# Hybrid retention and HGRN2 encoder step on 8 cores: two more x tiles loaded into the output tiles' buffers, and later landings assumed in the ordering

## The chip, the cores and the metric

The kernel runs on all 8 cores of one Trainium2 chip. Each core takes one of the 8 prompt streams and two of the 16 sample streams; the cores don't exchange data. The metric is device time in microseconds (us) of the slowest core, from the first to the last instruction and what lies around them. Lower is better.

## What is computed

One layer. For each of the 8 prompts (2048 frames of 1024 numbers) and 16 samples (16 frames each, with a running state):

```python
h = rmsnorm(x, g_pre)
u = h @ w_in                      # 1024 x 4096: eight segments of 512
rq, rk, rv, rg, hq, hf, hi, hg = split(u)
# head group A, retention, 4 heads of 128: rotary q and k, decay gamma per head
# head group B, HGRN2, 4 heads of 128: f = lb + (1-lb)*sigmoid(hf), k = 1-f, v = hi, q = silu(hq)
#   both: S_t = decay_t * S_(t-1) + k_t v_t^T,  o_t = q_t S_t, computed in chunks
o = concat(silu(rg) * headnorm(o_r), silu(hg) * headnorm(o_h))
y = x + rmsnorm(o @ w_out, g_post)
```

Outputs: y for prompts and samples, and the final states of both head groups.

## The kernel before, in words

**Tiling.** A core works on 16 prompt tiles of 128 frames, in four blocks of four tiles, and one sample tile of 48 rows (two streams of 16 frames at rows 0 and 32). All weights are held in SBUF as bf16: `Wi` (input, loaded by ten DMAs on GpSimd's queue at line 603 in the order of segments 0-1, 2-3, 4-5, 6-7) and `Wo` (output, two DMAs behind them). Most operations are recorded by name in these stages:

- `stage_A(k, j)` (line 648) for tile j of block k: x is loaded into a buffer by SP (line 662), ScalarE squares and sums it (line 670), GpSimd adds epsilon and takes the power (lines 673, 676), VectorE writes the normed tile `xbf` (line 679), and this is transposed into `xT`, on TensorE with a copy by ScalarE (lines 693, 697) in blocks 0 and 1, by a DMA transpose (line 685) in blocks 2 and 3. `xT` has two buffers, one a block.
- `stage_B_hg(k, h)` (line 753), head h of the HGRN2 group for a whole block: the projection of segment 5 (line 714), two ScalarE passes (lines 766, 768), forward scans on VectorE (line 773), a difference on GpSimd (line 781, `KTh`), more scans (line 785), the projection of segment 4, its SiLU (line 789) and a product on GpSimd (line 791, `QTh`). The scans' buffers `fG` and `fR` are double, `fQ` is single.
- `tile(k, j)` (line 1080): the rotary table's load, `stage_B_ret` (retention q and k: projections at line 731, rotary on VectorE, sums on GpSimd), `stage_C` (values and gates), `stage_D` (scores, outputs, state update; states `Sst` and `Sb`), `stage_E` (output projection at line 1009, norm, result in `xr`, stored by SP at line 1048). For all tiles but the last two `stage_E` lets a DMA of GpSimd's queue add x into `xr` (line 1031).

**The buffers in question.** x tiles are counted over the whole program, i = 0 to 16. `xs` and `xr` have two buffers each of 512 KB. Tile i goes to `xs[i % 2]`; only i = 2 and 3 go to `xr`, which `stage_E` otherwise uses for its results. So of block 1 (i = 4 to 7) tile 6 can be loaded only when tile 4 has been read, tile 7 when tile 5 has been read. The loads i = 4 and 5 also wait for the second half of segments 4 and 5 of `Wi` (key `('Wi', 5, 3)`).

**What sets the order.** The recorded order only gives the dependences (who writes and reads which name). The order of each engine's instructions, and of the DMAs that SP issues, is then chosen by a list scheduler (`list_schedule`, line 197) while the program is built. It keeps a planned time: each operation has a modelled cost and latency, a DMA is put through a model of the two queues (class `Net`), and at each step the operation that can start first is placed; among those that could start within 300 ns, the one with the higher priority (the longest chain behind it, plus a boost for early loads, plus noise of up to 500 from the seed `S.jitter`). PSUM banks are given out there too. When a DMA's modelled transfer ends, `landed` (line 250) makes its successors ready. On the chip nothing of the planned time is left, only the order on each engine and the semaphore waits: an engine that reaches an instruction whose data is not there stands, with all that is behind it.

`front(k)` (line 1065) records `stage_A` of the block's four tiles, the small set-up, and `stage_B_hg` for four heads; then the block's tiles follow. Block 1's `stage_A` is therefore recorded behind block 0's last `stage_E`. Filler matmuls (line 1128) are put into planned gaps of TensorE in the first 16 us.

Of the kernel before, what the change touches and what calls it, by code (L numbers as in the profile page):

```python
# [12 lines left out]
PE, ACT, DVE, POOL, SP = "pe", "act", "dve", "pool", "sp"  # L13
# [15 lines left out]
class Bank:  # L29
    def __init__(self, reserve):  # L30
        self.reserve = reserve
        self.idx = 0
# [45 lines left out]
class Sched:  # L78
    def __init__(self):
        self.ops = []  # L80
        self.last_w = {}
        self.readers = {}
        self.jitter = None

    def op(self, eng, fn, reads=(), writes=(), dma_key=None, deps=()):
        oid = len(self.ops)
        d = set(deps)
        for b in reads:
            w = self.last_w.get(b)
            if w is not None:  # L90
                d.add(w)
        for b in writes:
            w = self.last_w.get(b)
            if w is not None:
                d.add(w)
            d.update(self.readers.get(b, ()))
        d.discard(oid)
        self.ops.append(dict(eng=eng, fn=fn, deps=d, dma_key=dma_key, sig=False, sem=None, val=0, line=sys._getframe(1).f_lineno,
                             writes=tuple(writes), banks=[b for b in dict.fromkeys(tuple(reads) + tuple(writes)) if isinstance(b, Bank)]))
        for b in reads:  # L100
            self.readers.setdefault(b, []).append(oid)
        for b in writes:
            self.last_w[b] = oid
            self.readers[b] = []
        return oid
# [91 lines left out]
    def list_schedule(self):  # L197
# [16 lines left out]
        for i in range(n - 1, -1, -1):  # L214
            o = ops[i]
# [11 lines left out]
        XLAT = 110.0  # L227
# [5 lines left out]
        ready_t = [0.0] * n  # L233
# [16 lines left out]
        def landed(until):  # L250
            out = net.advance(until)
            for i, t in out:
                o = ops[i]
                t += o["lat"]
                o["t_land"] = t
                for sx in succ[i]:
                    ready_t[sx] = max(ready_t[sx], t + XLAT)
                    ndeps[sx] -= 1
                    if ndeps[sx] == 0:
                        avail[ops[sx]["eng"]].append(sx)  # L260
            return len(out)

        while done < n:
            best = None
            for e in ENGS:
# [4 lines left out]
                for i in avail[e]:  # L270
# [4 lines left out]
                    if v is not None:  # L275
                        k = free_bank(v)
# [15 lines left out]
            if landed(best[2] if best is not None else None):  # L292
                continue
# [4 lines left out]
            e, i, st_ = best  # L298
            o = ops[i]
            v = o["allocs"]  # L300
            if v is not None:
                k = free_bank(v)
# [189 lines left out]
def build_nc(limit=None, marks=None):  # L492
# [28 lines left out]
    with ExitStack() as st:  # L521
# [58 lines left out]
        def pbb(v):  # L580
            return psum[v.idx][:].bitcast(BF16)

        S = Sched()
# [64 lines left out]
        def stage_A(k, j):  # L648
            i = nA[0]
            nA[0] += 1  # L650
            slot = i % 2
            L = k.rows
            xbuf, xkey = xs[slot], ("xs", slot)
            if i in (2, 3):
                xbuf, xkey = xr[slot], ("xr", slot)
            if k.sample:
                S.op(POOL, lambda e: e.memset(xbuf[0:LS, :], 0.0), writes=[xkey])
                S.op(SP, lambda e: e.dma_start(out=xbuf[0:16, :], in_=xsm[0:16, :]), writes=[xkey], dma_key=("xsm", 0))
                S.op(SP, lambda e: e.dma_start(out=xbuf[32:48, :], in_=xsm[16:32, :]), writes=[xkey], dma_key=("xsm", 1))
            else:  # L660
                t0 = (k.b * 4 + j) * 128
                xid = S.op(SP, lambda e: e.dma_start(out=xbuf[:], in_=xp[t0:t0 + 128, :]), writes=[xkey], dma_key=xkey)
                if i < 4:
                    S.ops[xid]["boost"] = 20e6 - 1e6 * i
                elif i < 6:
                    S.ops[xid]["deps"].add(S.last_w[('Wi', 5, 3)])
            n0 = len(S.ops)
            junk, jk = (xbf[slot], [("xbf", slot)]) if i >= 4 else (gate[i], [("gate", i, 0), ("gate", i, 512)])
            sq = i % 4
            S.op(ACT, lambda e: e.activation(out=junk[0:L, :], in_=xbuf[0:L, :], func=AF.Square, scale=1.0 / 32,  # L670
                                             accum_out=ssx[0:L, sq:sq + 1]),
                 reads=[xkey], writes=[("ssx", sq)] + jk)
            S.op(POOL, lambda e: e.tensor_scalar(out=ssx[0:L, sq:sq + 1], in0=ssx[0:L, sq:sq + 1],
                                                scalar1=EPS, scalar2=None, op0=ALU.add),
                 reads=[("ssx", sq)], writes=[("ssx", sq)])
            S.op(POOL, lambda e: e.tensor_tensor(out=rsx[0:L, sq:sq + 1], in0=ssx[0:L, sq:sq + 1],  # L676
                                                 in1=mhalf[0:L, 0:1], op=ALU.pow),
                 reads=[("ssx", sq), "mhalf"], writes=[("rsx", sq)])
            S.op(DVE, lambda e: e.scalar_tensor_tensor(out=xbf[slot][0:L, :], in0=xbuf[0:L, :], scalar=rsx[0:L, sq:sq + 1],  # L679
                                                       in1=gpre[0:L, :], op0=ALU.mult, op1=ALU.mult),  # L680
                 reads=[xkey, ("rsx", sq), "gpre"], writes=[("xbf", slot)])
            if i == 3:
                first_norms.append(len(S.ops) - 1)
            if (k.b >= 2 and not k.sample):
                S.op(SP, lambda e: e.dma_start_transpose(out=k.xT[:, :, j * 128:(j + 1) * 128], in_=xbf[slot][:, :]),
                     reads=[("xbf", slot)], writes=[("xT", k.par, j)], dma_key=("xtr", slot))
            else:
                T = S.bank()

                def tr(e):  # L690
                    ins = None
                    for kc in range(8):
                        ins = e.transpose(out=pbb(T)[:, kc * L:(kc + 1) * L], in_=xbf[slot][0:L, kc * 128:(kc + 1) * 128],
                                          identity=ident[0:L, 0:L])
                    return ins
                S.op(PE, tr, reads=[("xbf", slot), "ident"], writes=[T, ("xT", k.par, j)])
                S.op(ACT, lambda e: e.activation(out=k.xT[:, :, j * 128:j * 128 + L],  # L697
                                                 in_=pbb(T)[:, 0:8 * L].rearrange("p (k l) -> p k l", k=8), func=AF.Copy),
                     reads=[T], writes=[("xT", k.par, j)])
            if i < 4:  # L700
                for o in S.ops[n0:]:
                    o["boost"] = 9e6 - 1e5 * i
# [34 lines left out]
        def lb_chain():  # L737
            S.op(DVE, lambda e: e.tensor_tensor(out=lbd[:], in0=lbt[:, 0, :], in1=lbt[:, 1, :], op=ALU.subtract),
                 reads=["lbt"], writes=["lbd"], deps=first_norms)
            S.op(ACT, lambda e: e.activation(out=lbd[:], in_=lbd[:], func=AF.Tanh, scale=0.5), reads=["lbd"], writes=["lbd"])  # L740
            S.op(DVE, lambda e: e.tensor_scalar(out=lbc[:, 0, :], in0=lbd[:], scalar1=0.25, scalar2=0.75, op0=ALU.mult, op1=ALU.add),
                 reads=["lbd"], writes=["lbc0"])
            S.op(DVE, lambda e: e.tensor_scalar(out=lbc[:, 1, :], in0=lbd[:], scalar1=-0.25, scalar2=0.25, op0=ALU.mult, op1=ALU.add),
                 reads=["lbd"], writes=["lbc1"])
# [312 lines left out]
        blocks = [prompt_block(b) for b in range(4)]  # L1057
# [5 lines left out]
            return rid  # L1063

        def front(k):
            for j in range(k.ns):
                stage_A(k, j)
            if k.b == 0:
                lb_chain()
            if k.sample or k.b < 2:  # L1070
                set_ret_dec(k)
            if k.sample:
                for i in range(NF):
                    S.op(POOL, lambda e, i=i: e.memset(fG[i][:, 0:2, 16:17], 1.0), writes=[("fG", i)] + [("fG", i, c) for c in range(1, 4)])
                S.op(POOL, lambda e: e.memset(k.QT[:, :, 0:LS], 0.0), writes=[("QT", k.par, h) for h in range(4)])
                S.op(POOL, lambda e: e.memset(k.KT[:, 0, :, 0:LS], 0.0), writes=[("KT", k.par, h) for h in range(4)])
            for h in range(4):
                stage_B_hg(k, h)
# [47 lines left out]

        def filler_fn(e, k):
            return e.matmul(psum[k][:, 0:128], lhsT=ident[:], rhs=ident[:], start=True, stop=True)
        S.jitter = (13, 500.0)
        S.emit(nc, st, filler=(filler_fn, ident_ready, 700.0, 400.0, 60.0, 16000.0, 1300.0, 6))  # L1130
    return nc

# [64 lines left out]
```

How the kernel before makes its waits and increments, by code:

```python
            def then_inc(self, *a, **k):  # L109
                return self
# [336 lines left out]
        def run(h, e):  # L447
            waited = {}
            for i in streams[e]:
                o = ops[i]
                req = {}
                for dpi in need[i]:
                    dp = ops[dpi]
                    key = id(dp["sem"])
                    if key not in req or req[key][1] < dp["val"]:
                        req[key] = (dp["sem"], dp["val"])
                for key, (sem, val) in req.items():
                    if waited.get(key, 0) >= val:
                        continue
                    h.wait_ge(sem, val)
                    waited[key] = val
                ins = o["fn"](h)
                if o["sig"]:
                    ins.then_inc(o["sem"], 16 if o["dma_key"] is not None else 1)
```

## Time and profile before

| | us |
|---|---|
| three runs | 381.78, 383.2, 438.44 |
| median | 383.2 |
| the profiled execution: time | 382.71 |
| its span on the slowest core (core 7) | 381.2 |
| spans of the 8 cores | 377.5 to 381.2 |
| TensorE, matmuls: busy | 357.4 (94%) |
| VectorE, ScalarE, GpSimd: busy | 237.9, 183.9, 218.7 |
| mean granted TensorE clock, core 7 | 0.991 |

One execution is profiled; the rows below are of its slowest core, in us from the span's start. PE is TensorE's matmuls, PEld its weight loads, DVE VectorE, ACT ScalarE, POOL GpSimd, SP the engine that issues most DMAs (SPq its queue). Matmuls overlap, so that the busy time of one is longer than what it adds to the total. A bracket behind a row of the timeline is the idle time of the engine just before it and what ended it.

### The profile page before, as it was taken

The numbers are of one execution on the slowest core, as the hardware profiler recorded it, in microseconds if no ns is written. First come the engines' busy times: TensorE is split into PE (matmuls) and PEld (weight loads), VectorE is DVE, ScalarE is ACT, GpSimd is POOL, SyncE is SP. The second block draws the span as 40 slices with busy tenths as digits, with TensorE's granted clock in tenths as the row PEclk, the third lists the DMA queues.
The fourth block names the chain that finished last, engine by engine and source line by source line (L and its number), as shares of the span: only waits on it lengthen the run. The fifth ranks groups of instructions, "written<-read, shape, count | busy, mean of one in ns | idle before, by whom it ended". The sixth has DMA issues, their size and how long they took to land.

```text
span 381.2 us, 8011 instructions; the slowest of 8 cores (377.5 to 381.2 us)
## 1 busy us (share of the span) xinstructions
PE 357.4 (94%) x2375; PEld 188.7 (50%) x2375; DVE 237.9 (62%) x524; ACT 183.9 (48%) x567; POOL 218.7 (57%) x292
## 2 busy tenths in 40 slices
PE   8989699689999999999979999999999999999993
PEld 8844354335455555444535454545454555545541
DVE  0137464684986975968656749486666464477545
ACT  2431242857878745463535252626353425435551
POOL 8425542557578776657446756575746365364630
PEclk9999899999999999999999999999999999999999
DMA  7999999997090997664566472525352556466714
GB/s 197 204 172 171 176 162 209 179 245 169 0 147 23 230 200 174 164 116 119 115 147 123 124 150 56 137 59 131 62 131 55 129 95 101 80 138 145 213 36 125
DMA packets 60619, 51.56 MB, mean 135 GB/s; under 512 B 41632, under 2 KB 48832, under 8 KB 60576
## 3 DMA queue, kind: packets, MB, share of 16 engines
q1 hardware_dynamic: 53104, 32.69, 34.4%
q0 software_dynamic: 7472, 18.35, 30.9%
q8 instruction: 20, 0.33, 0.4%
q14 instruction: 23, 0.19, 0.2%
HBM read 41.73 MB, written 10.09 MB: 136 GB/s over the span
## 4 chain that ended last, share of the span: by engine, by line
PE 62%; DMA 21%; POOL 5%; issue 5%; ACT 3%; DVE 3%; DVEq 0%; POOLq 0%; SPq 0%; ACTq 0%
PE bank L731 33%; PE bank L1009 14%; DMA Wi<-w_in 13%; PE bank L714 8%; DMA xs<-xp 5%; DMA xs<-sret 2%; PE bank L927 2%; PE bank L932 2%; PE bank L944 2%; PE bank L895 1%; POOL Wi L603 1%; DMA xT<-xbf 1%; DVE xbf L679 1%; POOL QTh L791 1%; POOL rsx L676 1%
## 5 line engine op out<-in xcount | busy, mean ns | idle before, releaser
L731 PE MATMUL bank<-Wi,xT 128*128 128x512 bf16 (+1 forms) x816 | 190.1, 381 | 1.7 <-ACT xT L697 0.7
L731 PEld LDWEIGHTS bank<-Wi,xT 128*128 128x128 bf16 (+1 forms) x816 | 77.5, 99 | 86.2 <-issue 6.0
L714 PE MATMUL bank<-xT,Wi 128*128 128x512 bf16 (+1 forms) x320 | 62.5, 342 | 4.8 <-POOL QTh L791 2.4
L965 DVE SCALAR_TENSOR_TENSOR og<-bank,rsq,gate 128x128 bf16<-128x128 f32 (+1 forms) x136 | 38.6, 343 | 43.9 <-POOL rsq L962 27.0
L1009 PE MATMUL bank<-Wo,ogT 128*128 128x512 bf16 (+1 forms) x272 | 62.8, 379 | 2.5 <-DVE Sst L949 2.5
L714 PEld LDWEIGHTS bank<-xT,Wi 128*128 128x128 bf16 x320 | 26.6, 98 | 36.5 <-issue 9.8
L1009 PEld LDWEIGHTS bank<-Wo,ogT 128*128 128x128 bf16 (+1 forms) x272 | 25.9, 98 | 31.2 <-issue 3.0
L884 POOL TENSOR_TENSOR Sst<-Sst,decS 128x512 f32<-128x512 f32 x30 | 31.4, 1049 | 16.4 <-DVE Sst L949 11.5
L955 ACT ACTIVATE og<-bank 128x128 bf16<-128x128 f32 (+1 forms) x136 | 35.5, 281 | 5.7 <-PE bank L927 3.7
L962 POOL TENSOR_TENSOR rsq<-ssq,mhalf 128x4 f32<-128x4 f32 (+1 forms) x34 | 34.7, 1021 | 4.4
L888 ACT ACTIVATE Sb<-Sst 128x512 bf16<-128x512 f32 x30 | 18.9, 630 | 36.7 <-POOL Sst L884 16.3
L854 ACT ACTIVATE gate<-bank 128x512 bf16<-128x512 f32 (+1 forms) x34 | 20.3, 598 | 30.0 <-PE bank L731 29.7
L781 POOL TENSOR_TENSOR KTh<-fG 128x512 bf16<-128x512 f32 (+1 forms) x20 | 18.8, 942 | 27.6 <-DVE fG L773 27.6
L773 DVE TENSOR_TENSOR_SCAN fG<-bank,zer 128x128 f32<-128x128 f32 (+1 forms) x72 | 23.3, 378 | 17.3 <-ACT bank L768 15.6
L679 DVE SCALAR_TENSOR_TENSOR xbf<-xs,rsx,gpre 128x1024 bf16<-128x1024 f32 (+1 forms) x15 | 22.5, 1511 | 17.7 <-POOL rsx L676 17.7
L819 POOL TENSOR_TENSOR qtm<-tA,tB 128x512 bf16<-128x512 f32 (+1 forms) x17 | 22.7, 1338 | 16.2 <-DVE tA L806 12.0
L1013 ACT ACTIVATE og<-bank 128x512 bf16<-128x512 f32 (+1 forms) x34 | 20.2, 595 | 22.8 <-PE bank L1009 22.8
L785 DVE TENSOR_TENSOR_SCAN fR<-bank,inv,zer 128x128 f32<-128x128 f32 (+1 forms) x72 | 28.0, 439 | 2.1 <-DVE inv L777 0.6
L955 ACT ACTIVATION_READ_ACCUMULATOR og<-bank 128x1 f32 (+1 forms) x136 | 29.0, 214 | 0.0
L791 POOL TENSOR_TENSOR QTh<-fQ,fR 128x512 bf16<-128x512 f32 (+1 forms) x20 | 22.8, 1140 | 8.8 <-ACT fQ L789 4.0
L819 POOL TENSOR_TENSOR Ktr<-tA,tB 128x512 bf16<-128x512 f32 (+1 forms) x17 | 22.5, 1322 | 8.5 <-DVE tA L806 6.2
L1027 DVE SCALAR_TENSOR_TENSOR xr<-bank,rs,gpost 128x512 f32<-128x512 f32 x30 | 21.5, 742 | 9.2 <-PE bank L714 4.8
(97 smaller groups left out, 457.9 us busy)
## 6 DMA issues: line engine op xcount, KB each, us to landing
xr<-xp POOLq DMA_DIRECT2D x15, 512.0 KB, 6.1
yp<-xr SPq DMA_DIRECT2D x15, 512.0 KB, 3.6
xs<-xp SPq DMA_DIRECT2D x14, 512.0 KB, 7.0
Wi<-w_in POOLq DMA_DIRECT2D x6, 1024.0 KB, 45.6
Wi<-w_in POOLq DMA_DIRECT2D x4, 512.0 KB, 19.0
Wo<-w_out POOLq DMA_DIRECT2D x2, 1024.0 KB, 73.8
xr<-xp SPq DMA_DIRECT2D x3, 512.0 KB, 11.2
rot<-rot_p SPq DMA_DIRECT2D x16, 96.0 KB, 6.3
```

The lines of the kernel that those rows point to most:

```text
L679: S.op(DVE, lambda e: e.scalar_tensor_tensor(out=xbf[slot][0:L, :], in0=xbuf[0:L, :], scalar=rsx[0:L, sq:sq + 1], in1=gpre[0:L, :], op0=AL ...
L714: ins = e.matmul(pb(v)[:, 0:nt], lhsT=Wi[:, kc, col0:col0 + 128], rhs=k.xT[:, kc, 0:nt], start=(kc == 0), stop=(kc == 7))
L731: ins = e.matmul(pb(v)[0:L, :], lhsT=k.xT[:, kc, j * 128:j * 128 + L], rhs=Wi[:, kc, seg * 512:(seg + 1) * 512], start=(kc == 0), stop=(kc ...
L773: S.op(DVE, lambda e, c=c: e.tensor_tensor_scan(out=G[:, c, rsl(cl - 1, cl)], data0=pb(v)[:, rsl(c * st_ + cl - 1, cl)], data1=zer[:, 0:cl ...
L785: S.op(DVE, lambda e, c=c: e.tensor_tensor_scan(out=pack(R)[:, c, :], data0=pb(v)[:, c * st_:c * st_ + cl], data1=zer[:, 0:cl], initial=IV ...
L791: S.op(POOL, lambda e: e.tensor_tensor(out=tok(k.QT[:, h, :]), in0=pack(SQ), in1=pack(R), op=ALU.mult), reads=["fQ", ("fR", f)] + [("fR", ...
L819: S.op(POOL, lambda e, ts=ts, dst=dst: e.tensor_tensor(out=dst[0:L, :], in0=tA[ts][0:L, :], in1=tB[ts][0:L, :], op=ALU.add), reads=[("tA", ...
L884: S.op(POOL, lambda e, Sst=Sst, cc=cc, g=g, gsl=gsl: e.tensor_tensor(out=Sst[:, gsl].rearrange("p (h e) -> p h e", h=4), in0=Sst[:, gsl].r ...
L955: S.op(ACT, lambda e, q_=q_, h=h, vo=vo: e.activation(out=ogs[vs][0:L, h * 128:(h + 1) * 128], in_=pb(vo)[0:L, q_ * 128:(q_ + 1) * 128], f ...
L962: S.op(POOL, lambda e, gq=gq, g=g: e.tensor_tensor(out=rsq[vs][0:L, gq], in0=ssq[vs][0:L, gq], in1=mhalf[0:L, 0:4], op=ALU.pow), reads=[(" ...
L965: S.op(DVE, lambda e, q_=q_, h=h, vo=vo: e.scalar_tensor_tensor(out=ogs[vs][0:L, h * 128:(h + 1) * 128], in0=pb(vo)[0:L, q_ * 128:(q_ + 1) ...
L1009: ins = e.matmul(pb(y)[0:L, :], lhsT=ogT[:, kc, 0:L], rhs=Wo[:, kc, n * 512:(n + 1) * 512], start=(kc == 0), stop=(kc == 7))
```

## The change

Four edits, in `Sched`, `stage_A`, `front` and the end of `build_nc`. Tiles i = 6 and 7 are loaded into `xr[0]` and `xr[1]`. Their loads, like those of i = 4 and 5, wait for `('Wi', 5, 3)`. `stage_A` of block 1's four tiles is recorded right behind block 0's four, ahead of block 0's heads and outputs, so that in `xr` the x tiles 6 and 7 come before the results of block 0; `front` of block 1 no longer records them. In the scheduler, what depends on an operation of SP or on a DMA transpose becomes ready 3000 ns later in planned time. The seed of the noise goes from 13 to 10.

```diff
@@ class Sched, __init__
+        self.slack = 0.0
@@ list_schedule, landed
-                    ready_t[sx] = max(ready_t[sx], t + XLAT)
+                    ready_t[sx] = max(ready_t[sx], t + XLAT + (self.slack if o["eng"] == SP or o["tr"] else 0.0))
@@ stage_A
-            if i in (2, 3):
+            if i in (2, 3, 6, 7):
                 xbuf, xkey = xr[slot], ("xr", slot)
...
-                elif i < 6:
+                elif i < 8:
                     S.ops[xid]["deps"].add(S.last_w[('Wi', 5, 3)])
@@ front
-            for j in range(k.ns):
-                stage_A(k, j)
+            if k.b != 1:
+                for j in range(k.ns):
+                    stage_A(k, j)
             if k.b == 0:
+                for j in range(4):
+                    stage_A(blocks[1], j)
                 lb_chain()
@@ build_nc
-        S.jitter = (13, 500.0)
+        S.slack = 3000.0
+        S.jitter = (10, 500.0)
```

## Rows read from the trace of the kernel before

**Rows 1.** The page, part 1: busy us (share of the span) xinstructions
```profile
PE 357.4 (94%) x2375; PEld 188.7 (50%) x2375; DVE 237.9 (62%) x524; ACT 183.9 (48%) x567; POOL 218.7 (57%) x292
```

**Rows 2.** The chain that ended last, in order of time: start us, us, what
```profile
8.37 48.39 DMA Wi<-w_in
...
101.49 3.45 PE bank L714 x16
...
113.37 0.76 DVE xr L1027
...
179.81 8.20 DMA xs<-sret
...
370.97 3.62 PE bank L1009 x16
```

**Rows 3.** Groups by shape: busy us, mean ns of one, idle before and releasers
```profile
L731 PE MATMUL bank<-Wi,xT 128*128 128x512 bf16 x768 | 178.7, 381 | 1.7 <-ACT xT L697 0.7 <-DMA Wi<-w_in 0.6 <-DVE Sst L952 0.4
...
L714 PE MATMUL bank<-xT,Wi 128*128 128x512 bf16 x256 | 59.9, 381 | 4.8 <-POOL QTh L791 2.4 <-DVE fR L785 2.1 <-ACT V L851 0.3
```

**Rows 4.** Windows: length, busy us of PE, PEld, DVE, ACT, POOL, clock, DMA share, GB/s
```profile
60.00:80.00 20.00, 15.89 (x92) 7.46 (x90) 13.11 (x34) 12.03 (x20) 8.11 (x9) 1.00 1.06 205
...
200.00:240.00 40.00, 40.00 (x234) 20.10 (x233) 28.47 (x63) 17.07 (x59) 26.14 (x30) 1.00 0.55 113
```

**Rows 5.** Timeline of TensorE, 20 to 130 us: start us, us, instruction, idle before it
```profile
71.52 0.61 PE L693 MATMUL bank<-ident,xbf 128*128 128x128 bf16 x8 [0.86 <-DVE xbf L679]
74.23 1.89 PE L714 MATMUL bank<-xT,Wi 128*128 128x512 bf16 x8 [2.11 <-DVE fR L785]
...
83.87 1.89 PE L714 MATMUL bank<-xT,Wi 128*128 128x512 bf16 x8 [1.53 <-POOL QTh L791]
```

**Rows 6.** Timeline of all engines, 174 to 200 us
```profile
192.50 1.06 ACT L670 ACTIVATE xbf<-xs 48x1024 bf16<-48x1024 f32 x1 [3.29 <-DMA xT<-xbf]
...
197.02 1.89 PE L1009 MATMUL bank<-Wo,ogT 128*128 128x512 bf16 x8 [2.52 <-DVE Sst L949]
```

**Rows 7.** Timeline of all engines, 56 to 92 us
```profile
66.88 1.06 ACT L670 ACTIVATE xbf<-xs 128x1024 bf16<-128x1024 f32 x1 [3.20 <-DMA xs<-xp]
...
69.45 0.74 DVE L773 TENSOR_TENSOR_SCAN fG<-bank,zer 128x128 f32<-128x128 f32 x2 [4.03 <-ACT bank L768]
...
83.80 1.06 ACT L670 ACTIVATE xbf<-xs 128x1024 bf16<-128x1024 f32 x1 [1.72 <-DMA xs<-xp]
```

**Rows 8.** Timeline of SP's queue: the loads of x tiles 4 to 8
```profile
56.93 0.90 SPq L662 DMA_DIRECT2D xs<-xp  x2
...
71.55 0.33 SPq L662 DMA_DIRECT2D xs<-xp  x1
...
84.87 0.33 SPq L662 DMA_DIRECT2D xs<-xp  x1
```

**Rows 9.** SP's waits in 70 to 72 us: us in total, times, longest
```profile
SPq L460 <- DVE xbf L679: 13.5, 1, 13.5
```

**Rows 10.** DMA in 57.5 to 71.4 us (two rows), then 71.5 to 84 us
```profile
DMA packets 1185, 2.84 MB, mean 204 GB/s; under 512 B 62, under 2 KB 62, under 8 KB 1184
...
q1 hardware_dynamic: 288, 1.05, 24.5%
...
q1 hardware_dynamic: 343, 1.27, 30.6%
```

**Rows 11.** Tile Wo: its loads (ns, first and last start) and their landing
```profile
L603 POOL DMA_DIRECT2D Wo<-w_out x2: 777/781/785, 10.7 to 11.4; - x2
...
DMA to landing us min/median/max: 69.6/73.8/78.1
```

**Rows 12.** Tile Wi: its loads and their landing
```profile
L603 POOL DMA_DIRECT2D Wi<-w_in x10: 741/781/965, 2.0 to 9.9; - x10
...
DMA to landing us min/median/max: 14.1/33.6/62.2
```

## The prediction

> **What bounds the kernel now.** I read the page first. TensorE is busy for 94% of the span and no other engine is above 62% [rows 1], so TensorE sets the time and the question is where it lacks work. Busy time hides that, because matmuls overlap. Sixteen 512-wide matmuls in a row pass in 3.45 us in the chain [rows 2], 0.216 us each, while the busy column charges 381 ns for one [rows 3]. The 1024 full matmuls of the input projections [rows 3] are therefore 1024 x 0.216 = 221 us of streaming where the busy column has 238.6 us. So I walked TensorE's timeline and took for each group its start plus its count x 0.216 us (0.0555 us for a 128-wide one, from the same timeline); what is left to the next start is a gap.
>
> Outside four places there is none worth having. Of 200 to 240 us TensorE is busy for 40.00 of 40 us, of 60 to 80 us for 15.89 of 20 us [rows 4]. The gaps are:
> - up to 57 us: the order waits for weights. The last quarter of the third piece of the input weights lands at 56.8 us (8.37 + 48.39 us) [rows 2], and by then TensorE has done nearly all that needs no later piece. Whatever order is written, this part ends near 57 us.
> - 57 to 92 us: the three largest waits shown are 0.86, 2.11 and 1.53 us [rows 5]; with the latency hidden behind each, and the smaller ones, the gaps are 8 us.
> - 194.3 to 197.0 us: 2.7 us, shown as a wait of 2.52 us [rows 6].
> - the end: the last large group starts at 370.97 us [rows 2]; of it 1.0 us is gaps between dependent steps, and 6.6 us after it is a dependent tail that no order removes.
>
> With 0.5 us at 124 us that is about 12 us after 57 us that an order could give back, out of a profiled time of 382.7 us (span 381.2 us and 1.5 us around it). The median of the three runs is 383.2 us, 0.5 us above the profiled one.
>
> **What makes the gap at 57 to 92 us.** The heads of the HGRN2 part of block 0 are computed there: projection, two ScalarE passes, scans on VectorE, a product on GpSimd. ScalarE's next instruction in its order is the sum of squares of x tile i = 4 (the first of block 1), and it waits 3.20 us for that tile to land, until 66.88 us [rows 7]. The two passes of the next head stand behind it, VectorE idles 4.03 us for them [rows 7], and TensorE then runs short before 71.5 and 74.2 us [rows 5]. Before 83.80 us it waits again, 1.72 us, for the fourth tile [rows 7], and about as long before 80.25 us for the third. These were issued late: SP issues two loads at 56.93 us, then waits 13.5 us for the buffer of the first, and issues the third at 71.55 us [rows 8, 9].
>
> **Part 1, other buffers for tiles three and four of block 1.** Nothing is added in instructions or bytes: two 512 KB loads go to xr instead of xs. What goes is SP's wait of 13.5 us. They can be issued beside the first two at about 58 us. What is late next is the DMA engines: in 57.5 to 71.4 us the hardware queue moved 1.05 MB and in 71.5 to 84 us 1.27 MB [rows 10], 75 and 102 GB/s, beside the weights. Four tiles are 2.1 MB: at 75 GB/s the last lands at 57 + 28 = 85 us, at 102 GB/s at 57 + 20.6 = 77.6 us. Before it was about 83.8 us (the fourth's reader starts at 83.80 us as the tile lands). So the fourth tile moves between 1 us later and 6 us earlier; I take 2 us, nearer to the row with a short queue, since that is the row in which these loads would run. Tile three, by the same count, lands at 78 us in place of 80.2 us. What that is worth on TensorE: at least 0, since TensorE could be fed by the heads of block 0 alone, and at most the 2 us of gaps behind 80 us. I take 1 us.
>
> The Trainium skill, DMA: Bandwidth & Descriptors, section Queues, rings and completion order, says that each DMA engine goes round-robin between the queues it has work for, a packet at a time. By that rule a queue with four loads in it draws no larger share than one with two, the lower rate holds, and part 1 gives 0 us. The trace agrees only in part: the queue's share of the engines rose from 24.5% to 30.6% [rows 10] when more was in it.
>
> The block's outputs now write the buffers that these tiles hold. The first such write is at 113.37 us [rows 2], over 20 us after the tiles have been read: no cost. If that cover went, each us of lateness would go onto the output of tile 0, which TensorE does not wait for.
>
> The xs buffers come free earlier, so tiles one and two of block 2, loaded before from 84.87 us on [rows 8], can be loaded from about 71 us on. That is 1 MB more beside the last weights. The output weights, issued last at 11.4 us, take at most 78.1 us to land [rows 11], so 89.5 us; 1 MB at the 204 GB/s of 57.5 to 71.4 us [rows 10] would be 5 us. The first matmul that reads them runs at 107.6 us, so 0 on the path.
>
> **Part 2, the 3 us of slack.** It adds no instruction. Whatever follows a load, a store or a transpose issued by SP (not the adding DMAs of GpSimd's queue) is put later in its engine's order, behind work that is ready. Two measured stalls are of the kind that it moves. First, ScalarE's 3.20 us at 66.88 us and the smaller ones after it: if the sum of squares stands behind the next head's passes, the head chain goes on. That is worth between 0 and the 3.20 us plus 2 us behind; I take 3 us, near the row itself. Second, the 2.7 us at 194 us. There SP issues a state load at 179.81 us and stands 8.20 us for it [rows 2] before it issues the next into the same buffer; the transpose behind it on SP goes out late, ScalarE waits 3.29 us for it, and at the end of that chain TensorE 2.52 us [rows 6]. With landing planned later, the transpose, the output store and the next transpose would stand ahead of the second state load. I take 2 us of 2.7 us.
>
> **Part 3, the order drawn anew.** The noise seed, the slack and the earlier places in program order each change the whole order of 8011 instructions. No row prices this. The nearest are the present gaps: in 250 us of steady work one stall of 2.7 us and one of 0.5 us. Bounds: 3 us gained, if they go by luck, to two or three new stalls like the largest, 8 us lost. I take 2 us lost, a stall somewhat below the one seen.
>
> **Sum.** -1 - 3 - 2 + 2 = -4 us: 382.7 becomes 378.7 us in a profiled run, and 0.5 us more, rounded, 379 us as a median.
>
> **The rivals.**
> - Absorbed. The head chain of block 0 is bound by its own steps (two buffers for the scans, VectorE between them), so the waits of ScalarE only change their name, and the stall at 194 us turns up elsewhere. For it: TensorE waits for VectorE's scans for 2.11 us at 74.23 us [rows 5], not for x. Against it: the 4.03 us in which VectorE itself had nothing. It gives 382 to 384 us.
> - All of it. Every gap after 57 us but about 2 us goes, 10 us less: 373 us. For it: steady stretches are full already. Against it: the gaps at 57 to 92 us are a dependent chain while the weights still land.
> - Slower: weights crowded out. With four block 1 tiles at once and two of block 2 from 71 us on, up to three tiles' bytes (1.5 MB) run ahead of the last input weights. These were issued last at about 9.9 us and take at most 62.2 us [rows 12], so land at 72 us; 1.5 MB at 204 GB/s is 7.4 us. If they land after about 77 us, when TensorE has only those products left, it stalls for the rest, and one drawn stall comes on top: +5 us, up to +7.4 us, so 388 to 390 us. Against it: the hardware queue held a fairly steady share, so loads wait behind each other more than weights behind them.
> - The change doesn't do what it says: SP's order puts the two loads after something else that waits, and they go out at 70 us anyway. Then only parts 2 and 3 count: 380 us, within the forecast's own range.
>
> **How the numbers follow.** Forecast 0.50 (374.5 to 383 us), absorbed 0.20, all of it 0.13, crowded out 0.12, loads not early 0.05. The range that leaves out no more than two in ten runs from 372.5 to 388.5 us: down to all of it, up to most of the crowded case. A change of 2% (7.7 us) is about what a measurement of this kernel tells from none: faster than 375.5 us is all of it and the lower edge of the forecast, 0.17; slower than 390.9 us is the far end of the crowded case with new stalls, 0.10; the rest is 0.73.
>
> **What would show it.** Right: four loads of x issued by SP within about 3 us after 56.9 us with no 13.5 us wait; ScalarE without a wait over 1 us for x at 63 to 67 us; the product of the last head of block 0 (before at 86.7 us) some 3 us earlier; SP without an 8 us stand between state loads, and no TensorE gap there; steady stretches at 40.0 of 40 us. Wrong: the last quarter of the weights landing over 3 us later; or gaps of more than 3 us in all after 100 us, which would say that the drawn order costs more than the slack saves.

## The result, and the profile after

The changed kernel takes 378.07 us (median of 4 runs, 378.03 to 378.85) against 382.7 us before (381.78 to 383.2): a ratio of 0.988, 95% interval 0.986 to 0.990. One of the four runs before (438.44 us) was in the chip's slower state, at a lower granted clock, and is left out, as such runs are in every median below. The forecast was 379.0 us, 4 us less than before; 4.6 us less were measured. The sum was right and its terms came near in size, but the reason given for the largest fell, and that the redrawn order cost no more is luck.

The page of the changed kernel, parts 1 and 2 (line numbers are higher by 1 than before up to `front`):

```profile
span 376.5 us, 7940 instructions; the slowest of 8 cores (373.7 to 376.5 us)
...
PE 357.6 (95%) x2343; PEld 188.3 (50%) x2343; DVE 234.8 (62%) x524; ACT 183.5 (49%) x567; POOL 218.5 (58%) x292
...
PEclk9989799999999999999999999999999999999997
DMA  7999999999521979653958346362393464465407
```

Against [rows 1] the busy times are the same within 1.3%, and the 32 matmuls fewer are all fillers (203 against 235): no work was taken away. The page doesn't say where 4.7 us of span went. The windows do. First the kernel before, then the one after, for the 35 us behind the landing of the third piece of the input weights (columns as in rows 4):

```profile
57.00:92.00 35.00, 29.18 (x170) 14.02 (x169) 22.16 (x46) 19.11 (x33) 17.58 (x18) 0.98 0.99 205
```
```profile
57.00:92.00 35.00, 34.35 (x206) 17.08 (x204) 24.65 (x57) 23.84 (x47) 20.82 (x24) 1.00 1.07 217
```

TensorE begins 36 more matmuls in the same stretch. To put all kernels on one scale I keep a ledger for each core: the matmuls begun up to a time, without the fillers, the full ones at 0.216 us and the 128-wide ones at 0.0555 us; the time less this is what TensorE had lost by then (waits and slow clock together). Here is the count to 92 us of the kernel after: all, the fillers, and the lines 732 and 715.

```profile
0.00:92.00 92.00, 82.40 (x603) 48.22 (x604) 46.79 (x100) 40.85 (x84) 49.57 (x71) 0.94 1.04 192
...
0.00:92.00 92.00, 15.71 (x203) 14.98 (x203) 0.94 1.04 192
...
0.00:92.00 92.00, 42.12 (x168) 16.29 (x168) 0.94 1.04 192
...
0.00:92.00 92.00, 17.78 (x80) 7.66 (x81) 0.94 1.04 192
```

168 + 80 = 248 full ones are 53.6 us; the other 603 - 203 - 248 = 152 are 8.4 us; 92 - 62.0 = 30.0 us lost. (The table below takes the larger of matmuls and weight loads for each count, since some records are missing: 29.8 us.) Lost by TensorE, slowest core of each, in us:

| | to 57 | 57 to 92 | to 92 | 92 to 335 | span |
|---|---|---|---|---|---|
| before | 26.4 | 7.7 | 34.1 | 4.4 | 381.2 |
| after | 28.6 | 1.2 | 29.8 | 3.4 | 376.5 |

So 4.3 us come from before 92 us, 1.0 us from the long middle, and the end gives 0.6 us back (4.3 + 1.0 - 0.6 = 4.7). The cores of one kernel differ by up to 6 us in what they have lost by 57 us (24.5 to 30.3 us over all kernels). In the kernel before, most of that difference is gone by 84 us (24.7 to 28.6 us become 32.6 to 33.7 us), so the column to 92 us is the one to compare. In the changed kernel it is not gone: its cores have lost 25.3 to 28.6 us by 57 us and 26.9 to 29.8 us by 92 us. The slowest core alone therefore tells too little, and the medians of the eight cores are given beside it: lost to 92 us 33.4 before and 28.2 us after; from 92 to 335 us 1.7 and 3.4 us. On six of eight cores the long middle has become worse, not better; what hides that on the slowest is told below, with the stall at 194 us.

SP's queue in the kernel after, x tiles 4 to 9:

```profile
56.82 0.91 SPq L663 DMA_DIRECT2D xs<-xp  x2
57.88 0.89 SPq L663 DMA_DIRECT2D xr<-xp  x2
72.33 4.84 SPq L663 DMA_DIRECT2D xs<-xp  x2
```

Four loads within 1.5 us, without the wait of 13.5 us [rows 8, 9]. Their readers on ScalarE:

```profile
67.98 1.05 ACT L671 ACTIVATE xbf<-xs 128x1024 bf16<-128x1024 f32 x1
...
71.72 1.05 ACT L671 ACTIVATE xbf<-xs 128x1024 bf16<-128x1024 f32 x1
...
77.74 1.06 ACT L671 ACTIVATE xbf<-xr 128x1024 bf16<-128x1024 f32 x1 [1.53 <-DVE fG L774]
...
79.70 1.04 ACT L671 ACTIVATE xbf<-xr 128x1024 bf16<-128x1024 f32 x1
```

No wait for x is left (before: 3.20 and 1.72 us [rows 7]), and the last product of block 0's heads starts at 82.59 us, 4.1 us earlier than the 86.69 us of before. The landing times of the four loads, then of all pieces of `Wi`, then of `Wo` (min, median, max):

```profile
DMA to landing us min/median/max: 8.8/12.8/17.1
...
DMA to landing us min/median/max: 15.1/34.5/67.4
...
DMA to landing us min/median/max: 77.4/80.1/82.7
```

The last x tile lands by 58.3 + 17.1 = 75.4 us where before it was 83.8 us. The weights take up to 5 us longer than in [rows 11, 12]: the last of `Wi`, issued at 8.8 us, lands by 76.2 us (before 72.1 us), and behind 57 us TensorE waits for none of them.

The stall at 194 us is gone as well, but it had been a matter of two cores. Spans before, by core:

```profile
core 0: 377.8 us, clock 0.990
core 1: 380.3 us, clock 0.986
...
core 3: 377.5 us, clock 0.988
...
core 7: 381.2 us, clock 0.991
```

Cores 1 and 7, on which SP got the first state load's landing late (SP issues the second at 187.27 and 188.08 us, on the others between 184.3 and 185.7 us), waited on TensorE 2.48 and 2.52 us before the output projection; the other six not over 0.2 us. They are the two slowest. So of the 4.4 us that core 7 lost in the middle 2.5 us are this stall and 1.9 us the rest, as on the other cores. Against those 1.9 us the kernel after loses 3.4 us, and no single wait of TensorE that the trace shows there is over 0.4 us.

SP's order in the kernel after has two transposes, the sample tile's among them, ahead of the second state load. The prediction had foreseen this for the sample's transpose, and for the output store, which stays behind:

```profile
176.00 0.39 SPq L1100 DMA_DIRECT2D xs<-sret  x1
...
181.46 1.22 SPq L686 DMA_TRANSPOSE xT<-xbf  x1
182.78 0.60 SPq L1100 DMA_DIRECT2D xs<-shg  x1
```

### The profile page after: what moved, and what is told of

It reads as the page before. It is cut to its first block, busy times and chain, and to the rows that moved or that the text cites. A ratio compares the mean times of both kernels' runs of the same rounds, so it can differ in the third digit from the quotient of the medians.

```text
span 376.5 us, 7940 instructions; the slowest of 8 cores (373.7 to 376.5 us)
## 1 busy us (share of the span) xinstructions
PE 357.6 (95%) x2343; PEld 188.3 (50%) x2343; DVE 234.8 (62%) x524; ACT 183.5 (49%) x567; POOL 218.5 (58%) x292
## 3 DMA queue, kind: packets, MB, share of 16 engines
q0 software_dynamic: 7472, 18.35, 32.6%
## 4 chain that ended last, share of the span: by engine, by line
PE 78%; DMA 10%; DVE 4%; POOL 3%; ACT 2%; issue 2%; DVEq 0%; POOLq 0%; ACTq 0%
PE bank L732 44%; PE bank L715 15%; PE bank L1010 12%; DMA Wi<-w_in 10%; PE bank L928 2%; PE bank L933 2%; PE bank L945 1%; PE bank L896 1%; ACT og L956 1%; POOL Wi L604 1%; POOL rsq L963 1%; DVE fR L786 1%; PE bank L997 1%; DVE Sst L950 1%; DVE xs L950 1%
## 5 line engine op out<-in xcount | busy, mean ns | idle before, releaser
L966 DVE SCALAR_TENSOR_TENSOR og<-bank,rsq,gate 128x128 bf16<-128x128 f32 (+1 forms) x136 | 38.8, 343 | 39.9 <-POOL rsq L963 36.5
L715 PE MATMUL bank<-xT,Wi 128*128 128x512 bf16 (+1 forms) x320 | 61.9, 340 | 0.4 <-DVE AT L904 0.3
L715 PEld LDWEIGHTS bank<-xT,Wi 128*128 128x128 bf16 x320 | 26.7, 97 | 31.3 <-issue 3.4
L963 POOL TENSOR_TENSOR rsq<-ssq,mhalf 128x4 f32<-128x4 f32 (+1 forms) x34 | 34.5, 1018 | 4.6 <-POOL ssq L960 0.4
L782 POOL TENSOR_TENSOR KTh<-fG 128x512 bf16<-128x512 f32 (+1 forms) x20 | 17.5, 877 | 33.4 <-DVE fG L774 31.7
L680 DVE SCALAR_TENSOR_TENSOR xbf<-xs,rsx,gpre 128x1024 bf16<-128x1024 f32 (+1 forms) x13 | 16.6, 1280 | 17.2 <-POOL rsx L677 17.2
L950 DVE TENSOR_TENSOR Sst<-bank,Sst 128x512 f32<-128x512 f32 x30 | 20.3, 684 | 11.0 <-PE bank L945 6.5
```

The costliest lines, as they stand in the source:

```text
L715: ins = e.matmul(pb(v)[:, 0:nt], lhsT=Wi[:, kc, col0:col0 + 128], rhs=k.xT[:, kc, 0:nt], start=(kc == 0), stop=(kc == 7))
L950: S.op(DVE, lambda e, vd=vd, Sst=Sst, gsl=gsl: e.tensor_tensor(out=Sst[:, gsl], in0=pb(vd)[:, :], in1=Sst[:, gsl], op=ALU.add), reads=[vd, ...
L963: S.op(POOL, lambda e, gq=gq, g=g: e.tensor_tensor(out=rsq[vs][0:L, gq], in0=ssq[vs][0:L, gq], in1=mhalf[0:L, 0:4], op=ALU.pow), reads=[(" ...
L966: S.op(DVE, lambda e, q_=q_, h=h, vo=vo: e.scalar_tensor_tensor(out=ogs[vs][0:L, h * 128:(h + 1) * 128], in0=pb(vo)[0:L, q_ * 128:(q_ + 1) ...
```

## The experiments

All were timed in rounds against the kernel before. A ledger of all of them stands behind the last.

**late_loads: the changed kernel, its order kept, the early loads taken back.** The waits are added after the scheduler has run, so that no instruction changes its place.

```diff
+            for i_, d_ in self.after:          # in emit, behind add_fillers
+                ops[i_]["deps"].add(d_)
...
+            norms[i] = len(S.ops) - 1          # in stage_A, behind the norm
+            if i in (6, 7, 8, 9):
+                S.after.append((xid, norms[i - 2]))
```

> The changed kernel, every engine's order kept, with waits added behind the scheduler: the loads of x tiles 6 to 9 wait for the norms of tiles 4 to 7, as they did before. Theory 1 (the slack's order pays, the early loads give little): the two loads go out near 71 us, tile 7 lands near 84 us, and the loss in 57 to 92 us rises from 1.2 us by at most 2 us: 378 to 380 us. Theory 2 (the early loads pay): the heads' order now finds its x late, 57 to 92 us loses 5 us or more again: 382 to 384 us. Theory 3 (the draw pays, not one of the two parts): no change, 378 us.

Measured 387.7 us, 9.6 us more than the changed kernel and 1.4% over the kernel before (interval 1.010 to 1.019). ScalarE and TensorE in 76 to 92 us:

```profile
85.64 1.06 ACT L675 ACTIVATE xbf<-xr 128x1024 bf16<-128x1024 f32 x1 [9.47 <-DMA xr<-xp]
...
88.06 3.57 PE L739 MATMUL bank<-Wi,xT 128*128 128x512 bf16 x8 [6.62 <-ACT xT L705]
```

One wait of 9.47 us becomes 6.62 us on TensorE. The changed order relies on the early loads; theory 2 was not even high enough. One reason is that the run goes further than back: in the changed order the norms that the two loads wait for come later, so that both go out at 76.9 us, where the kernel before issued them at 71.55 and 75.4 us. What this doesn't say is that the loads make the gain: an order planned for early data is worse than the old one when the data comes late.

**early_same_order: the other way round, the early loads in the order of before.** The two loads go to `xr`, their waits are exchanged after scheduling, and block 0's outputs wait for the readers.

```diff
+            for i_, add_, drop_ in self.swap:  # in emit, behind add_fillers
+                ops[i_]["deps"] = (ops[i_]["deps"] - drop_) | add_
...
+            if i in (6, 7):                    # in stage_A
+                xbuf = xr[slot]
+                S.swap.append((xid, {S.last_w[('Wi', 5, 3)], norms[i - 4]}, {norms[i - 2], norms[i - 2] - 3, xld[i - 2]}))
+                for d_ in outs[i - 6]:
+                    S.swap.append((d_, {len(S.ops) + 3}, set()))
```

> The kernel before with every engine's order kept; the third and fourth loaded x tile of block 1 go to xr (their loads no longer wait for the norms of the first two, and block 0's first two outputs wait for their readers). If the early loads pay by themselves: they go out at 57 to 59 us, the ScalarE waits before 80.25 and 83.80 us and the two TensorE gaps behind them (1.7 us at 82 us, part of the 2.3 us at 72 us) shrink, 380 to 381 us. If they pay only in an order that was planned for them: within 1 us of before, 382.5 us. If four loads at once crowd the weights: slower, 384 us.

Measured 381.48 us, ratio 0.9968 (0.9935 to 1.0001): about 1 us, hardly told from none. The loads do what they do in the changed kernel (SP's queue, then ScalarE and TensorE):

```profile
57.70 1.03 SPq L666 DMA_DIRECT2D xs<-xp  x2
58.79 0.98 SPq L666 DMA_DIRECT2D xr<-xp  x2
```
```profile
66.71 1.06 ACT L680 ACTIVATE xbf<-xs 128x1024 bf16<-128x1024 f32 x1 [2.71 <-DMA xs<-xp]
...
79.82 1.06 ACT L680 ACTIVATE xbf<-xr 128x1024 bf16<-128x1024 f32 x1
```
```profile
74.07 3.40 PE L725 MATMUL bank<-xT,Wi 128*128 128x512 bf16 x8 [2.11 <-DVE fR L796]
```

The landed tiles wait for their place in the order: the third is squared at 79.82 us, nearly as late as before (80.25 us), though the fourth comes at 81.53 us instead of 83.80 us, and TensorE's wait of 2.11 us for the scans [rows 5] is still there. Of the three forecasts the second, within 1 us of before, comes nearest.

**buffers_only and slack_only: one part each, seed 13.** Edits: the changed kernel with `S.slack = 0.0` and seed 13; the kernel before with the slack of 3000.

> The kernel before with the xr buffers and the earlier recording of block 1's first stage, seed 13, no slack. Theory 1 (slack pays): still waits of ScalarE of 2 to 4 us for x tiles in 57 to 84 us, about 382 us. Theory 2 (early loads pay): 378 to 379 us. Theory 3 (draw): anywhere in 378 to 386 us, with new gaps after 100 us.

Measured 386.79 us, ratio 1.012 (1.007 to 1.016).

> The kernel before with the 3 us of slack alone, seed 13. Theory 1 (slack pays): no ScalarE wait over 1 us for x in 57 to 84 us, about 379 us. Theory 2 (early loads pay): the loads of x tiles 6 and 7 still go out after 70 us, 57 to 92 us loses 6 us or more, 382 to 383 us. Theory 3 (draw): anywhere in 378 to 386 us, with new gaps after 100 us.

Measured 388.14 us, ratio 1.015 (1.010 to 1.019). Each part alone is slower than neither, and both times lie above everything that the three theories allowed (386 us at most). But the two lose in different places. TensorE in 57 to 84 us, buffers alone, then slack alone:

```profile
57.00:84.00 27.00, 22.99 (x122) 10.80 (x121) 17.15 (x37) 14.71 (x26) 8.60 (x13) 0.94 1.05 209
```
```profile
57.00:84.00 27.00, 25.67 (x143) 12.33 (x145) 17.95 (x45) 16.38 (x29) 10.44 (x12) 1.00 1.07 204
```

With the slack 21 more matmuls have begun by 84 us, though the last two x tiles arrive as late as before (their readers run at 82.8 and 86.2 us). ScalarE waits 4.26 us for x with buffers alone, not at all up to 84 us with the slack alone. What slack_only has won by 84 us it loses again, and more, until 120 us: in 92 to 120 us TensorE is busy for 22.6 of 28 us at a granted clock of 0.94, and by 120 us it has lost 38.4 us where the kernel before has lost 34.8 us and the changed kernel 31.1 us.

**act_move and early_act_move: the one instruction that the prediction blamed.** In the order of before, the sum of squares of the first loaded x tile of block 1 is put two places back, behind the next head's two passes. (That tile is i = 5; SP loaded it ahead of i = 4, which the prediction named.)

```diff
+            for e_, i_, n_ in self.moves:      # in emit, behind add_fillers
+                q_ = order[e_]
+                p_ = q_.index(i_)
+                q_.insert(p_ + n_, q_.pop(p_))
...
+            if i == 5:                         # in stage_A, behind the sum of squares
+                S.moves.append((ACT, len(S.ops) - 1, 2))
```

> The kernel before with one instruction moved, nothing else: the sum of squares of the first x tile of block 1 stands behind the next head's two ScalarE passes instead of ahead of them. If ScalarE's wait of 3.20 us for that tile caused the gaps up to 75 us: the head's scans start 4 us earlier and the loss in 57 to 92 us falls from 7.7 us by 2 to 4 us, 379 to 381 us. If the wait only changes its name (the x tile or the scans' buffers bound it anyway): within 1 us of before.

Measured 382.1 us, ratio 0.9997 (0.997 to 1.003): nothing. ScalarE's wait there falls from 3.20 to 0.96 us, and the next stops stay:

```profile
67.66 1.06 ACT L675 ACTIVATE xbf<-xs 128x1024 bf16<-128x1024 f32 x1 [0.96 <-DMA xs<-xp]
...
80.26 1.06 ACT L675 ACTIVATE xbf<-xs 128x1024 bf16<-128x1024 f32 x1 [1.75 <-DMA xs<-xp]
...
83.83 1.06 ACT L675 ACTIVATE xbf<-xs 128x1024 bf16<-128x1024 f32 x1 [1.74 <-DMA xs<-xp]
```

The third and fourth tile are squared at the same times as before, within 0.03 us; so what the wait had delayed was not what came last. The eight cores of the kernel before say the same without any edit. Their waits at this instruction differ from 0.72 to 5.06 us; cores 0 and 1:

```profile
66.35 1.06 ACT L670 ACTIVATE xbf<-xs 128x1024 bf16<-128x1024 f32 x1 [5.06 <-DMA xs<-xp]
...
66.00 1.06 ACT L670 ACTIVATE xbf<-xs 128x1024 bf16<-128x1024 f32 x1 [0.82 <-DMA xs<-xp]
```

By 92 us the first has lost 33.2 us, the second 33.5 us.

> As early_same_order, and with the first sum of squares of block 1 behind the next head's two passes (act_move, which alone gave nothing). If the two waits hid each other: 378 to 380 us, the loss in 57 to 92 us falls from 7.7 us by 3 to 5 us. If the order around them has to change as well: as early_same_order.

Measured 380.7 us, ratio 0.995 (0.992 to 0.997). With both the early loads and the move 2 us are there, 0.9 us of it lost less by 92 us than before; the interval overlaps that of early_same_order, so the move's own share is not shown. What the changed kernel has beyond that comes with an order that differs in more than one place.

**both_seed13, both_seed11, no_slack, seed_only: the draw apart from the parts.** Edits: the seed in the changed kernel; its slack at 0; the seed 10 in the kernel before.

> The changed kernel with the old seed 13: both parts, another draw. If the two parts together make the gain (they need each other): 377 to 380 us, the loss in 57 to 92 us 1 to 3 us. If the draw makes it: 57 to 92 us may be as good, but new gaps after 92 us of 5 us or more, 383 to 388 us, as in the kernels with one part each (386.8 and 388.1 us).

Measured 382.52 us, ratio 1.000 (0.998 to 1.003), between the two forecasts: the front is good again (30.2 us lost by 92 us), and what is won there goes in the middle and at the end.

> The changed kernel with the slack at 0, seed 10. If the slack makes its share of the gain: ScalarE waits again for x tiles between 60 and 84 us, 57 to 92 us loses 4 us or more, 381 to 386 us. If buffers and seed make it: 378 to 379 us. Either way a new draw can cost up to 8 us after 92 us, which the ledger by stretches shows apart.

Measured 384.7 us, ratio 1.004 (1.001 to 1.007), as expected if the slack makes its share of the gain. ScalarE's wait is back (3.23 us before 67.35 us), and TensorE's with it:

```profile
72.30 0.61 PE L694 MATMUL bank<-ident,xbf 128*128 128x128 bf16 x8 [2.66 <-DVE xbf L680]
74.70 3.57 PE L715 MATMUL bank<-xT,Wi 128*128 128x512 bf16 x8 [0.80 <-DVE fR L786]
```

> The kernel before with seed 10 and nothing else: what a draw is worth by itself. Neither part is in, so the loss in 57 to 84 us should stay at 6 to 7 us (as in the three kernels without slack); after 92 us anything from 3 to 8 us. 381 to 388 us. If it is 378 us, the seed and not the two parts makes the gain.

Measured 386.33 us, ratio 1.008 (1.005 to 1.011): the new seed by itself is worse than the old one.

> The changed kernel with seed 11, a third draw beside 10 (378.1 us) and 13 (382.5 us). If slack acts on 57 to 84 us whatever the draw: loss there 1 to 3.5 us. After 92 us the draw decides: 3 us as with seed 10, or 8 to 11 us as with seed 13. 378 to 385 us.

Measured 387.67 us, ratio 1.012 (1.009 to 1.015), above the 378 to 385 us expected. Up to 92 us this kernel is as good as the changed one. It then loses 8.5 us, and its end is 5 us longer. TensorE there:

```profile
373.47 0.35 PE L997 MATMUL bank<-ident,og 48*128 48x48 bf16 x8 [1.50 <-DVE og L966]
374.56 5.24 PE L1010 MATMUL bank<-Wo,ogT 128*48 128x512 bf16 x16 [0.73 <-ACT ogT L1000]
```

The last output projection takes 5.24 us after those waits where it took 3.62 us before [rows 2]; the granted clock in 375 to 386 us is 0.81.

**front_slack13, front_slack10: the slack only up to 95 us of planned time.**

```diff
-(self.slack if o["eng"] == SP or o["tr"] else 0.0)
+(self.slack if (o["eng"] == SP or o["tr"]) and t < 95000.0 else 0.0)
```

> Both parts, seed 13, the slack only for DMAs that land before 95 us of planned time. If the slack helps where loads share the engines with the weights and its delays cost the steady part (after 92 us the two kernels with slack and seed 13 lose most): 57 to 84 us loses 1 to 3.5 us and after 92 us some 4 us, 378 to 380 us. If the losses after 92 us are the draw and not the slack: 382 us or more again.

Measured 384.4 us, ratio 1.005 (1.002 to 1.007): some 2 us slower than with the slack throughout.

> As front_slack13, seed 10 (the changed kernel with slack cut off after 95 us of planned time). 57 to 92 us as in the changed kernel (1 to 2 us lost), since nothing in the planning differs up to there. After 92 us: if the slack is of use or neutral there, 378 to 380 us; if it costs, 376 to 377.5 us.

Measured 379.02 us, ratio 0.989 (0.986 to 0.993), not to be told from the changed kernel. The idea that the slack costs the steady part has nothing for it; a further draw decides again. No version here beats the changed kernel.

**The ledger.** Lost by TensorE in us, slowest core of each; "end" is the span less what was lost up to 335 us, that is the work, the same in all, and whatever is lost at the end. The column "8 cores" has the median of the eight cores for "to 92" and, in brackets, their range. Each row is one profiled execution.

| | slack | early loads | to 92 | 8 cores | 92 to 335 | end | median us |
|---|---|---|---|---|---|---|---|
| before | no | no | 34.1 | 33.4 (32.8 to 34.1) | 4.4 | 342.7 | 382.7 |
| act_move | no | no | 34.1 | 33.5 (31.5 to 34.8) | 2.7 | 343.3 | 382.1 |
| seed_only | no | no | 35.2 | 34.5 (33.4 to 36.3) | 6.6 | 343.1 | 386.33 |
| buffers_only | no | yes | 35.2 | 34.2 (31.9 to 35.2) | 7.9 | 343.1 | 386.79 |
| no_slack | no | yes | 34.8 | 33.4 (31.3 to 34.8) | 5.3 | 342.9 | 384.7 |
| early_same_order | no | yes | 33.7 | 32.2 (30.6 to 33.7) | 1.6 | 343.0 | 381.48 |
| early_act_move | no | yes | 33.2 | 32.5 (30.2 to 33.2) | 2.8 | 343.2 | 380.7 |
| late_loads | yes | taken back | 38.1 | 36.5 (36.1 to 38.1) | 5.0 | 343.1 | 387.7 |
| slack_only | yes | no | 30.8 | 30.8 (all 30.8) | 9.3 | 345.8 | 388.14 |
| after | yes | yes | 29.8 | 28.2 (26.9 to 29.8) | 3.4 | 343.3 | 378.07 |
| both_seed13 | yes | yes | 30.2 | 30.2 (30.2 to 30.8) | 5.1 | 345.2 | 382.52 |
| both_seed11 | yes | yes | 29.6 | 29.4 (28.5 to 30.6) | 8.5 | 348.3 | 387.67 |
| front_slack13 | front | yes | 30.2 | 30.4 (30.2 to 31.4) | 9.5 | 342.9 | 384.4 |
| front_slack10 | front | yes | 30.6 | 28.6 (26.9 to 30.6) | 4.1 | 343.2 | 379.02 |

Two things can be read off. The column to 92 us falls into two groups: 33.2 to 35.2 us without slack, 29.6 to 30.8 us with it (late_loads apart, whose loads don't come when its plan has them). The medians of the eight cores fall into the same two groups, 32.2 to 34.5 us and 28.2 to 30.8 us; single cores of the two overlap between 30.2 and 31.4 us. Three pairs differ in the slack alone: no_slack and after (seed 10), buffers_only and both_seed13, before and slack_only (seed 13). It is worth 5.0, 5.0 and 3.3 us on the slowest core and 5.2, 4.0 and 2.6 us in the medians. So the slack is worth 3 to 5 us at the front, with both seeds that were run with and without it; seed 11 was run only with it. Seed and buffers move the column less, up to 2 us. The columns behind it, 1.6 to 9.5 us and up to 5.6 us at the end, follow neither part: with both parts the middle loses 3.4 to 9.5 us, without either 2.7 to 6.6 us. They are what differs between orders that are otherwise equal in kind, and they are as large as the gain. Of the end one can say that the three kernels over 345 us are among the four planned with slack to the last instruction, and that the one pair that differs in this alone (both_seed13 and front_slack13) has 2.3 us less end for 4.4 us more middle; that is too little to call it shown.

## Why the prediction was right, point by point

- **TensorE is the bound: right.** Every kernel but the three with the longer end has the same work and end within 0.6 us, 342.7 to 343.3 us, and time follows the gaps. That 12 us of gaps behind 57 us are all that an order can give was not reached by any version, and stays an estimate.
- **Part 1, when the tiles land: mis-sized.** Forecast 77.6 to 85 us for the last, 82 taken; it was 75.4 us, outside the bounds. The step that failed is the rate, 75 GB/s, taken from a mean over 57.5 to 71.4 us [rows 10]. In that stretch the hardware queue moved nothing before 60 us and nothing after 69.5 us. Where both queues had work, in 62 to 66 us, it moved 0.63 MB in 4 us, 158 GB/s, and in the kernel after 0.66 MB, 165 GB/s; what four loads change is that it has work for longer. The Trainium skill's rule (DMA: Bandwidth & Descriptors, Queues, rings and completion order) of turns between queues, a packet at a time, from which the prediction took that a longer queue draws no larger share, agrees with these rows; the last section has them in packets. What failed was the step from there to "the lower rate holds".
- **Part 1, what it is worth: 1 us, right in the order of before** (0.9968, some 1.2 us, with an interval that touches none), **and too small inside the changed order,** where taking the early loads back costs 9.6 us (with loads that go out even later than before). A term of such a sum holds only for the order in which it is measured.
- **The outputs of block 0 don't wait, the later weights cost nothing: right.** No row of the kernel after has TensorE waiting for weights behind 57 us, though the last of `Wi` lands 4.1 us later, at 76.2 us. The slower rival put its stall at a landing after about 77 us, so it was missed by less than 1 us.
- **Part 2, ScalarE's wait: the size nearly right, the reason wrong.** I took 3 us for putting one instruction back. The slack does give 3 to 5 us by 92 us, but the step "the head chain goes on if the sum of squares stands behind the next passes" failed: with just that, the time stayed (0.9997). The "absorbed" rival was right about that single wait. (The tile it waits for is i = 5, not i = 4.) What the slack changes is the order of many instructions at once in this stretch; which of them are needed was not separated further.
- **Part 2, the stall at 194 us: gone, 2.5 us on the slowest core for 2 us taken.** It was on two of eight cores only, which the profile of the slowest alone could not show. The order that was foreseen, the sample's transpose ahead of the second state load, stands in three of the four plans with slack to the end (not in both_seed11) and in none without. But that it ends the stall is not shown: act_move keeps SP's order of before and has no wait over 1 us there on any core, early_same_order one of 1.42 us on one core. The stall comes and goes with one landing, and undoing it by itself was not tried.
- **Part 3, the draw: 2 us lost, right for this order, by luck.** With the stall taken by itself, core 3 after loses 1.5 us more in the middle than core 7 before (3.4 against 1.9 us) and 0.6 us more at the end, 2.1 us together; the medians of the eight cores have 1.7 us more in the middle. It is not one new stall, as priced, but many short waits. Nothing in the prediction could know it: both_seed11, the same two parts with another seed, loses 6.6 us more in the middle and 5.6 us more at the end than before without its stall, 12 us, beyond the bound of 8 us, and half of it in the end, a place for which I had allowed no new stall.
- **The sum.** By this account -4.3 us at the front (forecast -1 - 3), -2.5 us for the stall (-2) and +2.1 us for the draw (+2) make the 4.7 us of span. The sizes fit; what lies behind the front's 4.3 us is not what was written, and with another seed the same change gave 382.5 or 387.7 us. That the draw was near its middle value is luck.
- **The signs.** All those named as right came but one: 200 to 240 us has TensorE busy for 39.7 of 40 us, not 40.0. Both signs of being wrong came too: the last of `Wi` landed 4.1 us later, and after 100 us the cores lose 3.0 to 3.4 us up to 335 us. The first did no harm: TensorE waited for none of those weights. The second was read too strictly: it says that the order drawn costs about 2 us, not that it costs more than the 4 to 5 us saved at the front.
- **The chances.** 2% faster had 0.17 and needed all gaps to go; after 57 us this kernel still loses 4.6 us up to 335 us. The range, 372.5 to 388.5 us, holds all five orders with both parts or a front slack (378 to 388 us). It was about as wide as it had to be. Slower than 390.9 us had 0.10, too much even by the prediction's own slower rival, which ends at 390 us.

## What to carry to other kernels

When a static order comes from a planner, look for what the plan believes of its loads. Landings planned earlier than they come leave engines standing at instructions whose data is late. Here the scheduler of the kernel before (`t_land` in `list_schedule`) had the four tiles landed at 63.8, 67.6, 74.6 and 78.5 us of planned time; on the chip the first, third and fourth came at 66.9, 80.25 and 83.80 us. Moving a single such instruction may give nothing where a plan with later landings gives several microseconds. Before crediting a part of such a change, run it with two or three other seeds and keep a ledger by stretch and by core: here three seeds of the same plan differed by 9.6 us in total, twice the gain, while the part's own effect stood clear only in what was lost by 92 us. An order tuned for early data is also a dependence on it (9.6 us when it came late), so the two have to be kept or undone together.

## What the runs showed of the hardware

While both had work, the hardware queue (SP's loads) and the software queue (the weights) moved the same number of packets, as taking turns would give, whether the first had two 512 KB loads in it or four. In 62 to 66 us, before and then after:

```profile
q0 software_dynamic: 172, 0.35, 56.6%
q1 hardware_dynamic: 169, 0.63, 47.0%
```
```profile
q0 software_dynamic: 175, 0.34, 58.2%
q1 hardware_dynamic: 177, 0.66, 47.7%
```

Over the eight cores the hardware queue had 43.0% to 50.6% before and 41.8% to 48.8% after. The Trainium skill's rule of turns, cited above, would give the same. Four loads differ from two only in keeping the queue filled for longer: in 66 to 69.5 us core 7 before has 92 packets of it against 215 of the other, core 3 after 155 against 153. So over 57.5 to 71.4 us, a stretch that holds both kinds of time, the share rises from 22.6% to 25.5% before to 29.8% to 37.0% after. The row of the kernel after that answers to [rows 10]:

```profile
q1 hardware_dynamic: 450, 1.66, 33.9%
```

The price was paid by the other queue: over the eight cores its last piece of `Wi` landed 66.6 to 70.0 us after issue instead of 61.9 to 63.7 us, its last piece of `Wo` 82.7 to 85.3 us instead of 77.8 to 80.9 us. With the slack but without the early loads (slack_only) these were 63.6 to 65.4 us and 78.0 to 80.5 us. And between SP's two state loads, of which the second waits for the first, lay 5.3 to 6.2 us on six cores and 7.6 and 8.3 us on two, in one execution of one program; these two are the ones with the stall of 2.5 us.
